# Two encoder layers on eight cores: block products in the feed-forward, a convolution in phase layout, stages without barriers

## Chip, cores, metric

One Trainium2 chip, eight cores. Each core computes one sequence of the batch (4096 positions, 1024 channels) with its own copy of the weights; the cores exchange nothing. The metric is the device time in microseconds of the slowest core.

## What is computed

Matmul operands may be bf16; sums are float32. Per sequence:

```python
# D=1024, SEQ=4096, D_FF=2816
for l in (0, 1):
    h = rmsnorm(x, mix_norm_g[l])
    x = x + (even_mixer(h) if l == 0 else odd_mixer(h))
    h = rmsnorm(x, ffn_norm_g[l])
    x = x + (silu(h @ w_gate[l]) * (h @ w_up[l])) @ w_down[l]
return rmsnorm(x, final_norm_g)

# even_mixer: z = h @ w_in (1536 wide) -> a, gate, p (512 each)
#   ya = silu(layernorm(depthwise_conv31(a * sigmoid(gate)) + b))
#   yb = (mean over a centred window of 2/4/8/16 positions - p) @ pool_w * scale, per group of 128 channels
#   return concat(ya, yb) @ w_out
# odd_mixer: z = h @ w_in -> c, u, v (512 each)
#   yc = Re(DFT over positions and 128 channels of c) @ fourier_w, 4 heads
#   yd = gelu(u) * (W_s @ layernorm(gelu(v)) + b) in chunks of 128 positions
#   return concat(yc, yd) @ w_out
```

## The kernel before

Everything is written out instruction by instruction. Class K issues the work: `mm` (L107, the matmul itself is L111) issues a group of TensorE matmuls that share a PSUM bank, `op` (L100) one instruction of another engine, `dma` (L116, L119) transfers on the queue of SP or of POOL. Each operand has a Dep, and `_pre` (L75) makes the issuing engine wait for the last writer and readers. Engines work in the order of the program text. `run_pipeline` (L274) interleaves the stages of a loop over tiles of 128 positions. `barrier` (L138) makes every engine wait for all engines and all transfers; it stands after each stage, where SBUF memory is given to other tensors.

**mixer0** (L496), one stage after the other: `norm_phase` (L330) reads 32 tiles of x, squares and sums on ACT (L298), takes a root on ACT (L301) and a reciprocal on DVE (L304), scales on DVE (L308), transposes by eight matmuls against `ident` and evacuates into `bigA`; then the projections: a and gate (512 matmuls of 128x512), 124 diagonal weight matrices `diag` built by DVE (L546), p; pooling as matmuls against band matrices; the convolution as 31 matmuls for each of 32 blocks (8 groups of 512 positions times 4 of channels), each against one diagonal matrix that shifts by one tap, with layernorm over channels by matmuls against `ones`; the output projection `out_phase` (L345, add at L369).

**ffn_phase** (L378), once per layer: four supertiles `st` of 1024 positions. `gu(st)` (L406): for 22 columns of 128 hidden channels and 2 halves of 512 positions, eight matmuls for gate and eight for up, then silu on ACT (L430) and the product into `gT` on DVE (L432): 704 matmuls. The weights come as float32 and are cast by transfers on POOL's queue into `wgu`, three slots of 256 columns of gate and up, again for every supertile; `wd` is loaded once. `down_stages(st)` (L436): 8 tiles of 44 matmuls, added to the residual (L460) and stored, woven with the normalisation of the next supertile.

**mixer1** (L693): normalisation; c to memory (`cdr`), u; v with gelu (L775), statistics on DVE (L781, L784), normalisation on ACT (L803) and POOL (L807, L810), product with `swT`; the Fourier transform in three steps of matmuls with evacuations shared by ACT and DVE (`evac_on`, L872); output projection.

One block of gate:

```python
k.mm([(ps[:, bg, :], wgu[:, sl, 0, kk, jj * 128:(jj + 1) * 128],
       hT_[:, kk, tg * 512:(tg + 1) * 512], kk == 0, kk == 7) for kk in range(8)], ...)
```

## Time and profile before

| | us |
|---|---|
| median of 3 runs (3437.47 to 3456.11) | 3439.22 |
| profiled execution, span of the slowest core | 3426.9 |
| spans of the eight cores | 3407.2 to 3426.9 |
| TensorE busy in it | 2912.4 (85%) |
| DVE, ACT, POOL busy | 987.9, 833.8, 310.7 |

The span runs from the first to the last instruction of the core. The profiled execution's own device time isn't listed; the median of the runs is 12.3 us above its span, which is start and end around the instructions. All eight cores do the same, and their mean granted TensorE clock lies at 0.922 to 0.925 of full speed. Busy time of an engine says how long at least one instruction was in it; idle time counts only where it is TensorE's, or where TensorE waits for it.

### The profile page before, as it was taken

Reading aid. Unit: us, or ns where it says so; the run is one execution under the profiler, and the core shown is the slowest. Engines: PE = TensorE matmul, PEld = TensorE weight load, DVE = VectorE, ACT = ScalarE, POOL = GpSimd, SP = SyncE. Lnnn points to the kernel's source line nnn. Section 1 sums busy time; section 2 is a strip of 40 time slices with the busy share of each in tenths; the row PEclk is TensorE's granted clock in tenths of the full one; section 3 lists DMA queues with packets and bytes.
Section 4 is the critical chain, followed back from the end, with each engine's and each line's share of the span. In section 5 each row is a group of like instructions: output and inputs, shape, how many; then the busy total and the mean of one; then the engine's idle time right before and its main releaser. Section 6 shows DMA issues by size and latency. Waiting matters only on the chain.

```text
span 3426.9 us, 42073 instructions; the slowest of 8 cores (3407.2 to 3426.9 us)
## 1 busy us (share of the span) xinstructions
PE 2912.4 (85%) x14392; PEld 1376.4 (40%) x14392; DVE 987.9 (29%) x1566; ACT 833.8 (24%) x1515; POOL 310.7 (9%) x337
## 2 busy tenths in 40 slices
PE   2875999877999999999955966299599899899898
PEld 2433544333444444444433422164244444444444
DVE  5342322341122132221135044153212323323222
ACT  5211344111112211111025345230212212212211
POOL 0000122000101101101000033200110010010000
PEclk9987999988999999999976976599799999999999
DMA  8002000689645635536254000438965465454432
GB/s 217 26 1 34 2 1 1 205 264 165 81 120 103 81 136 88 86 114 81 53 157 157 30 1 1 101 114 286 208 87 110 113 76 122 105 74 123 80 50 80
DMA packets 259436, 336.74 MB, mean 98 GB/s; under 512 B 10784, under 2 KB 199840, under 8 KB 258464
## 3 DMA queue, kind: packets, MB, share of 16 engines
q0 software_dynamic: 196448, 117.62, 25.9%
q1 hardware_dynamic: 62784, 216.43, 18.5%
q8 instruction: 124, 2.03, 0.2%
q14 instruction: 80, 0.66, 0.1%
HBM read 380.31 MB, written 71.30 MB: 132 GB/s over the span
## 4 chain that ended last, share of the span: by engine, by line
PE 79%; DMA 7%; ACT 4%; DVE 4%; issue 4%; POOL 1%; DVEq 0%; SPq 0%; ACTq 0%; POOLq 0%
PE ps L111 79%; DMA sb_wgu<-ffn_w_up 3%; ACT sb_junk L298 2%; DMA sb_xin<-xres 2%; DVE sb_diag L546 1%; DMA sb_fw<-od_fourier_w 1%; ACT sb_vt L803 1%; DVE sb_hb L308 1%; DMA sb_xin<-x 1%; POOL sb_vt L807 1%; DMA sb_band<-band 1%; POOL sb_vn L810 1%; DVE sb_bst L781 0%; ACT sb_vt L775 0%; DMA xres<-sb_xout 0%
## 5 line engine op out<-in xcount | busy, mean ns | idle before, releaser
L111 PE MATMUL ps<-sb_h2T,sb_wgu 128*128 128x512 bf16 x5632 | 1237.6, 383 | 46.9 <-DMA sb_wgu<-ffn_w_up 46.9
L111 PEld LDWEIGHTS ps<-sb_h2T,sb_wgu 128*128 128x128 bf16 x5632 | 556.0, 99 | 725.4 <-issue 74.7
L111 PE MATMUL ps<-sb_wd,sb_gT 128*128 128x512 bf16 x2816 | 613.0, 379 | 10.8 <-DVE sb_gT L432 10.8
L432 DVE TENSOR_TENSOR sb_gT<-sb_tmp,ps 128x512 bf16<-128x512 f32 x352 | 242.1, 688 | 1041.2 <-PE ps L111 1023.6
L111 PE MATMUL ps<-sb_w_in,sb_bigA 128*128 128x512 bf16 x1792 | 426.6, 402 | 51.7 <-DVE sb_p_sb L560 35.7
L430 ACT ACTIVATE sb_tmp<-ps 128x512 f32<-128x512 f32 x352 | 210.1, 597 | 1027.4 <-PE ps L111 1027.3
L111 PEld LDWEIGHTS ps<-sb_wd,sb_gT 128*128 128x128 bf16 x2816 | 273.9, 98 | 339.2 <-issue 14.5
L111 PE MATMUL ps<-sb_ident,sb_hb 128*128 128x128 bf16 x1024 | 114.6, 281 | 237.5 <-DVE sb_hb L308 110.2
L111 PEld LDWEIGHTS ps<-sb_w_in,sb_bigA 128*128 128x128 bf16 x1792 | 180.2, 102 | 280.6 <-issue 89.0
L119 POOL DMA_DIRECT2D sb_wgu<-ffn_w_gate x88 | 77.6, 882 | 1978.4 <-PE ps L111 1643.3
L298 ACT ACTIVATE sb_junk<-sb_xin 128x1024 bf16<-128x1024 f32 x128 | 134.3, 1049 | 357.8 <-DMA sb_xin<-xres 347.3
L111 PE MATMUL ps<-sb_uT,sb_diag 128*128 128x512 bf16 x992 | 215.8, 379 | 1.9 <-DVE sb_bigA L613 1.9
L111 PEld LDWEIGHTS ps<-sb_ident,sb_hb 128*128 128x128 bf16 x1024 | 89.5, 126 | 267.1 <-issue 260.0
L111 PE MATMUL ps<-sb_bigA,sb_w_in 128*128 128x512 bf16 x768 | 168.0, 382 | 2.0 <-issue 2.0
L308 DVE SCALAR_TENSOR_TENSOR sb_hb<-sb_xin,sb_ssb,sb_gbc 128x1024 bf16<-128x1024 f32 x128 | 164.4, 1284 | 14.9 <-DVE sb_ssb L304 3.0
L460 DVE TENSOR_TENSOR sb_xout<-sb_xin,ps 128x1024 f32<-128x1024 f32 x64 | 78.0, 1218 | 233.3 <-PE ps L111 233.3
L111 PEld LDWEIGHTS ps<-sb_uT,sb_diag 128*128 128x128 bf16 x992 | 96.2, 97 | 120.3 <-issue 2.2
L369 DVE TENSOR_TENSOR sb_xout<-sb_xin,ps 128x1024 f32<-128x1024 f32 x64 | 78.2, 1221 | 149.7 <-PE ps L111 126.9
L111 PEld LDWEIGHTS ps<-sb_bigA,sb_w_in 128*128 128x128 bf16 x768 | 75.6, 98 | 94.1 <-issue 4.7
L321 ACT ACTIVATE sb_h2T<-ps 128x512 bf16<-128x512 f32 x64 | 38.1, 595 | 307.3 <-PE ps L111 306.8
L111 PE MATMUL ps<-sb_swT,sb_vn 128*128 128x128 bf16 x128 | 33.9, 265 | 69.6 <-POOL sb_vn L810 58.4
L324 DVE TENSOR_SCALAR sb_h2T<-ps 128x512 bf16<-128x512 f32 x64 | 44.1, 689 | 138.1 <-PE ps L111 138.1
(101 smaller groups left out, 1375.8 us busy)
## 6 DMA issues: line engine op xcount, KB each, us to landing
sb_xin<-xres SPq DMA_DIRECT2D x192, 512.0 KB, 5.5
xres<-sb_xout SPq DMA_DIRECT2D x96, 512.0 KB, 3.7
sb_wgu<-ffn_w_gate POOLq DMA_DIRECT2D x88, 512.0 KB, 6.4
sb_wgu<-ffn_w_up POOLq DMA_DIRECT2D x88, 512.0 KB, 8.3
sb_xin<-x SPq DMA_DIRECT2D x64, 512.0 KB, 5.7
out<-sb_xout SPq DMA_DIRECT2D x32, 512.0 KB, 3.0
sb_wd<-ffn_w_down POOLq DMA_DIRECT2D x4, 2816.0 KB, 73.8
sb_gbc<-norm_g SPq DMA_DIRECT2D x11, 512.0 KB, 4.4
```

Source lines behind the costliest of these rows:

```text
L111: ins = self.nc.tensor.matmul(o, lhsT=l, rhs=r, start=st, stop=sp)
L119: ins = q.e.dma_start(out=o, in_=i)
L298: k.op(act, lambda e: e.activation(out=junk[:], in_=xin[:, xs, :], func=AF.Square, accum_out=ssb[:, s_:s_ + 1]), reads=[d_xin[xs]], writes ...
L308: k.op(dve, lambda e: e.scalar_tensor_tensor(out=hb[:, h_, :], in0=xin[:, xs, :], scalar=ssb[:, s_:s_ + 1], in1=gbc[:, 0, :], op0=ALU.mult ...
L321: k.op(act, lambda e: e.activation(out=hT[:, 0:4, c0:c0 + 128], in_=psv[:, 0:4, :], func=AF.Copy, scale=float(np.sqrt(D))), reads=[psd[b]] ...
L324: k.op(dve, lambda e: e.tensor_scalar(out=hT[:, 4:8, c0:c0 + 128], in0=psv[:, 4:8, :], scalar1=float(np.sqrt(D)), scalar2=None, op0=ALU.mult),
L369: k.op(dve, lambda e: e.tensor_tensor(out=xout[:, xo, :], in0=xin[:, xs, :], in1=ps[:, b:b + 2, :].rearrange("p b n -> p (b n)"), op=ALU.add),
L430: k.op(act, lambda e: e.activation(out=tmp[:, ts_, :], in_=ps[:, bg, :], func=AF.Silu), reads=[psd[bg]], writes=[d_tmp[ts_]])
L432: k.op(dve, lambda e: e.tensor_tensor(out=gT[:, j, tg * 512:(tg + 1) * 512], in0=tmp[:, ts_, :], in1=ps[:, bu, :], op=ALU.mult), reads=[d_ ...
L460: k.op(dve, lambda e: e.tensor_tensor(out=xout[:, xo, :], in0=xin[:, xs, :], in1=ps[:, b:b + 2, :].rearrange("p b n -> p (b n)"), op=ALU.add),
L546: k.op(dve, lambda e: e.tensor_scalar(out=diag[:, c, tap, :], in0=identf[:], scalar1=cw[:, c, tap:tap + 1], scalar2=None, op0=ALU.mult), r ...
L803: k.op(act, lambda e: e.activation(out=vt[:, r_, h * 128:(h + 1) * 128], in_=vt[:, r_, h * 128:(h + 1) * 128], func=AF.Identity, scale=mv[ ...
```

## The change

All stages are rewritten. What it does, by stage:

- **Waits.** `barrier` is gone. SBUF has fixed addresses; `reg` makes a new tensor wait for the last users of exactly those bytes. TensorE no longer waits for its own semaphore.
- **Feed-forward.** The products of 1024 positions with the weights are taken as products of 2x2 blocks with seven block products instead of eight. The contraction (1024 into 2x512), the hidden channels (2x1408) and the positions (2x512) are halved; sums and differences of blocks stand in 7 parts: `hTs` (activations), `slot` (weights), `G` (hidden activations). `gu` has 22 groups (11 pairs of gate and up) of 28 matmuls of 128x512, that is 616, in 7 products of 4; ACT copies running sums out of PSUM (`snap`), DVE adds the other products (`addb`), ACT applies silu in SBUF, DVE multiplies (`mult`) and makes four sums of two bf16 parts (L325). `down` has 28 products of 11 matmuls, 308, each added to `X` in SBUF. The parts of the weights are made once per layer by `Prep`: 33 pieces, each 4 casting loads on POOL's queue, 4 sums and a store to memory; 24 pieces of layer 0 in mixer0 (sums on DVE), 9 in the first `gu` (on POOL), 21 of layer 1 in the next three `gu` (on POOL), 12 in mixer1 (on DVE). The supertiles then read bf16 parts by SP's queue into three slots: 10 loads of 1.84 MB, 2 of 0.92 and 7 of 1.44 per supertile.
- **mixer0.** Positions are ordered by phase (position modulo 8). Normalisation, projections and pooling run as one loop, one tile and 24 matmuls at a step. Pooling is adds on DVE (L325) without matmuls. The convolution runs on 32 groups of 16 channels times 8 phases: 5 matmuls each with matrices `CW` of 640 columns, made by POOL (8 ahead, 24 in the loop); u goes to memory and back for that. The layernorm's two halves run on DVE, POOL and ACT, the first before the output projection, the second woven into it; its result goes to memory and back. The pool weights are multiplied into `w_out`.
- **mixer1.** Normalisation, the three projections, the layernorm of v and the gating are one loop. The layernorm's affine part is on DVE (L1315). The first four tiles are normalised in the last `down` of layer 0.
- **Normalisation** everywhere: sum of squares on ACT (L451), then add and power -0.5 on POOL (L337, L325), then L457 on DVE; no root on ACT, no reciprocal on DVE. Its steps are woven into `down` and into the output projections, with the next stage's first tiles.

```diff
+PRD = {"P1": (0, 0), "P2": (1, 1), "P3": (6, 2), "P4": (2, 6), "P5": (3, 3), "P6": (4, 4), "P7": (5, 5)}
+
+GP = {0: 0, 1: 1, 4: 2, 5: 3, 3: 4, 6: 5, 2: 6}
+
+GL = []
+for _d in range(5):
+    GL += [(0, 2 * _d), (0, 2 * _d + 1), (1, 2 * _d), (1, 2 * _d + 1)]
+GL += [(0, 10), (1, 10)]
...
+                    seq = [(3, 5, 0, ALU.subtract), (4, 2, 3, ALU.subtract), (5, 2, 5, ALU.subtract),
+                           (6, 1, 4, ALU.subtract)]
+                    dst, dd = wds[l].rearrange("s p n -> p s n")[:, :, it[1] * 512:(it[1] + 1) * 512], d_wds[l][it[1]]
+                else:
+                    seq = [(3, 5, 2, ALU.add), (4, 3, 0, ALU.subtract), (5, 0, 5, ALU.subtract),
+                           (6, 1, 4, ALU.subtract)]
...
+                for o, a, c, op in seq:
+                    tt(self.eng, buf[:, o], buf[:, a], buf[:, c], op, d, d)
...
+                def snap(g, x):
+                    v = nx()
+                    grp[g][x] = v
+                    copy_on(act, X[:, v, :], ps[:, grp[g]["A"], :], [psd[grp[g]["A"]]], [dX[v]])
+
+                def addb(g, x, b):
+                    v = grp[g][x]
+                    tt(dve, X[:, v, :], X[:, v, :], ps[:, b, :], ALU.add, [dX[v], psd[b]], [dX[v]])
...
+                for g in range(NJ + 1):
+                    m = g - 1
...
+                        prod(g, "P1", grp[g]["A"], True)
+                        snap(g, "x1")
+                    if m >= 0:
+                        prod(m, "P7", grp[m]["A"], False)
+                        snap(m, "x3")
+                    if g < NJ:
+                        prod(g, "P2", grp[g]["B"], True)
+                        addb(g, "x1", grp[g]["B"])
+                        if not gate_g:
+                            mult(g, "x1", 0)
+                    if m >= 0:
+                        addb(m, "x3", grp[m]["C"])
+                        if not gate_m:
+                            mult(m, "x3", 2)
+                    if g < NJ:
+                        prod(g, "P6", grp[g]["A"], False)
+                        snap(g, "x2")
+                    for a in late:
+                        silu(*a)
+                    late = []
+                    if m >= 0:
+                        A_ = grp[m]["A"]
+                        prod(m, "P4", A_, False)
+                        if gate_m:
+                            v = nx()
+                            grp[m]["x4"] = v
+                            k.op(act, lambda e: e.activation(out=X[:, v, :], in_=ps[:, A_, :], func=AF.Silu),
+                                 reads=[psd[A_]], writes=[dX[v]])
+                            silu(m, "x3")
+                        else:
+                            s4 = grp[PART[m]]["x4"]
+                            jm = GL[m][1]
+                            tt(dve, G[:, GP[1], jm, :], X[:, s4, :], ps[:, A_, :], ALU.mult, [dX[s4], psd[A_]],
+                               [dG[1][jm]])
+                    if g < NJ:
+                        if gate_g:
+                            silu(g, "x1")
+                        prod(g, "P5", grp[g]["C"], True)
+                    if m >= 0:
+                        prod(m, "P3", grp[m]["C"], False)
+                        addb(m, "x2", grp[m]["C"])
+                        if gate_m:
+                            late.append((m, "x2"))
+                        else:
+                            mult(m, "x2", 5)
+                            jp = GL[m][1]
+                            for o, a, b, op in ((3, 5, 2, ALU.add), (4, 3, 0, ALU.subtract), (5, 0, 5, ALU.subtract),
+                                                (6, 1, 4, ALU.subtract)):
+                                tt(dve, G[:, GP[o], jp, :], G[:, GP[a], jp, :], G[:, GP[b], jp, :], op,
+                                   [dG[a][jp], dG[b][jp]], [dG[o][jp]])
...
+                def prod(p, i, b, s, first):
+                    wp = PRD[p][0]
+                    k.mm([(ps[:, b, :], G[:, GP[wp], j, i * 128:(i + 1) * 128],
+                           self.slot[s][:, j * 512:(j + 1) * 512], first and j == 0, j == HJ - 1) for j in range(HJ)],
+                         reads=[self.d_slot[s]] + dG[wp], writes=[psd[b]], more=not first)
...
+        def conv(g):
+            b = k.rot("cv", [0, 1, 2, 3])
+            s = g % NCW
+            k.mm([(ps[:, b, :], CW[s][:, o, :], U[:, g, o:o + NB], o == 0, o == 4) for o in range(5)],
+                 reads=[d_CW[s]] + d_Uq, writes=[psd[b]])
+            v = U[:, g, 2:2 + NB]
+            k.op(act, lambda e: e.activation(out=v, in_=ps[:, b, :], func=AF.Identity, bias=evp[:, g, 0:1]),
+                 reads=[psd[b], d_evp], writes=[d_v[g]])
+            k.op(act, lambda e: e.activation(out=vq[g % 4][:], in_=ps[:, b, :], func=AF.Square, bias=evp[:, g, 0:1]),
+                 reads=[psd[b], d_evp], writes=[d_vq[g % 4]])
+
+        def conv_stat(g):
+            k.mm([(ps[:, 6, :], sel[:], U[:, g, 2:2 + NB], g == 0, g == NG - 1)], reads=[d_sel, d_v[g]],
+                 writes=[psd[6]])
+            k.mm([(ps[:, 7, :], sel[:], vq[g % 4][:], g == 0, g == NG - 1)], reads=[d_sel, d_vq[g % 4]],
+                 writes=[psd[7]])
+
+        for g in range(NG + 2):
...
+        for T_ in range(1, 10):
+            for j in range(4):
+                u = 4 * T_ + j
+                w = u - 4
+                if u < NT:
+                    d_norm(u)
+                if w < NT:
+                    cproj(w)
+                    uproj(T_ - 1, j)
+                    vproj(w)
+                if 0 <= w - 1 < NT:
+                    cstore(w - 1)
+                    vstat(w - 1)
+                if 0 <= w - 2 < NT:
+                    vnorm(w - 2)
+                if 0 <= w - 4 < NT:
+                    sgu(w - 4)
+                if w >= 1 and w % 8 == 1 and w > 1:
+                    ctm_load((w - 9) // 8)
+                if w % 4 == 0 and w < NT:
+                    prep1.step()
```

On DVE, the gate and up part of the first supertile: before, one product per pair of banks (`gT`), between the normalisation and the first add of `down`.

```order
L304 RECIPROCAL sb_ssb<-sb_ssb 128x1
L308 SCALAR_TENSOR_TENSOR sb_hb<-sb_xin,sb_ssb,sb_gbc 128x1024
L324 TENSOR_SCALAR sb_h2T<-ps 128x4x128 x2
L432 TENSOR_TENSOR sb_gT<-sb_tmp,ps 128x512 x44
L460 TENSOR_TENSOR sb_xout<-sb_xin,ps 128x1024
L304 RECIPROCAL sb_ssb<-sb_ssb 128x1
L308 SCALAR_TENSOR_TENSOR sb_hb<-sb_xin,sb_ssb,sb_gbc 128x1024
```

And now, in the first gate and up part, where up groups follow gate groups (`X`: running sums in SBUF, `ps`: PSUM, `G`: the parts of the hidden activation):

```order
L325 TENSOR_TENSOR sb_X<-sb_X,ps 128x512
L325 TENSOR_TENSOR sb_G<-sb_X 128x512
L325 TENSOR_TENSOR sb_G<-sb_X,ps 128x512
L325 TENSOR_TENSOR sb_X<-sb_X,ps 128x512
L325 TENSOR_TENSOR sb_G<-sb_X 128x512
L325 TENSOR_TENSOR sb_G<-sb_G 128x512 x4
L325 TENSOR_TENSOR sb_X<-sb_X,ps 128x512 x2
L325 TENSOR_TENSOR sb_G<-sb_X 128x512
L325 TENSOR_TENSOR sb_G<-sb_X,ps 128x512
L325 TENSOR_TENSOR sb_X<-sb_X,ps 128x512
L325 TENSOR_TENSOR sb_G<-sb_X 128x512
L325 TENSOR_TENSOR sb_G<-sb_G 128x512 x4
```

Each of the 44 products `gT` before is replaced by adds from PSUM, multiplications, and, behind every up group, four sums of `G` with itself.

On PE, the convolution before (`uT`: gated input, `diag`: diagonal matrices, `vb`, `vq`: values and squares for the layernorm):

```order
L111 MATMUL ps<-sb_uT,sb_diag 128x512 x124
L111 MATMUL ps<-sb_vb,sb_ones 128x512 x4
L111 MATMUL ps<-sb_vq,sb_ones 128x512 x4
L111 MATMUL ps<-sb_uT,sb_diag 128x512 x124
L111 MATMUL ps<-sb_vb,sb_ones 128x512 x4
L111 MATMUL ps<-sb_vq,sb_ones 128x512 x4
```

And now (`CW`: phase matrices, `sel`: the sum over channels):

```order
L160 MATMUL ps<-sb_U,sb_CW 128x512 x5
L160 MATMUL ps<-sb_U,sb_sel 128x512
L160 MATMUL ps<-sb_vq,sb_sel 128x512
L160 MATMUL ps<-sb_U,sb_CW 128x512 x5
L160 MATMUL ps<-sb_U,sb_sel 128x512
L160 MATMUL ps<-sb_vq,sb_sel 128x512
L160 MATMUL ps<-sb_U,sb_CW 128x512 x5
```

Where 124 matmuls stood per 512 positions there are 5 per group of 16 channels, 160 for 992 in all, and the 64 for the layernorm are spread between them.

On PE in mixer1, where normalisation had ended before; c and u, then v and the gating:

```order
L111 MATMUL ps<-sb_bigA,sb_w_in 128x512 x256
L111 MATMUL ps<-sb_w_in,sb_bigA 128x512 x56
L111 MATMUL ps<-sb_swT,sb_vn 128x128
L111 MATMUL ps<-sb_sbrow,sb_ones_row 128x128
L111 MATMUL ps<-sb_swT,sb_vn 128x128
L111 MATMUL ps<-sb_sbrow,sb_ones_row 128x128
```

And now, in the loop (`hb` the normalised tile, `w_in` and `hT` the projections, `sbrow` and `swT` the gating):

```order
L160 MATMUL ps<-sb_ident,sb_hb 128x128 x8
L160 MATMUL ps<-sb_w_in_13157,sb_hT_13161 128x512 x8
L160 MATMUL ps<-sb_hT_13161,sb_w_in_13157 128x512 x8
L160 MATMUL ps<-sb_w_in_13157,sb_hT_13161 128x512 x8
L160 MATMUL ps<-sb_sbrow,sb_ones_row 128x512
L160 MATMUL ps<-sb_swT,sb_vn 128x128 x4
L160 MATMUL ps<-sb_ident,sb_hb 128x128 x8
```

The transposes of one tile, 24 projection matmuls of the tiles before it and a gating step now follow one another.

## Rows read from the trace of the kernel before

**Rows 1.** The page: busy time by engine; the chain that ended last, by engine.

```profile
PE 2912.4 (85%) x14392; PEld 1376.4 (40%) x14392; DVE 987.9 (29%) x1566; ACT 833.8 (24%) x1515; POOL 310.7 (9%) x337
...
PE 79%; DMA 7%; ACT 4%; DVE 4%; issue 4%; POOL 1%; DVEq 0%; SPq 0%; ACTq 0%; POOLq 0%
```

**Rows 2.** Stages: stretch, its length, busy of PE, PEld, DVE, ACT, POOL, clock, DMA, GB/s.

```profile
230.00:313.00 83.00, 45.84 (x203) 20.11 (x201) 39.04 (x115) 7.76 (x13) 0.90 (x2) 0.77 0.00 1
...
366.00:624.50 258.50, 229.80 (x1056) 101.87 (x1057) 53.56 (x49) 99.19 (x136) 60.03 (x65) 0.98 0.00 1
...
740.00:837.00 97.00, 51.98 (x256) 25.52 (x256) 24.38 (x36) 24.64 (x46) 12.71 (x14) 0.74 1.06 199
837.00:1757.00 920.00, 892.64 (x4224) 408.44 (x4224) 200.55 (x268) 149.34 (x266) 66.40 (x76) 0.99 0.48 93
1757.00:1857.00 100.00, 32.40 (x257) 24.84 (x258) 64.94 (x96) 61.53 (x129) 1.76 (x2) 0.51 0.74 209
...
1980.00:2180.00 200.00, 126.40 (x464) 49.38 (x462) 77.44 (x279) 96.06 (x178) 83.47 (x70) 0.67 0.02 3
2180.00:2223.00 43.00, 4.52 (x37) 3.60 (x38) 2.07 (x3) 6.84 (x25) 0.49 (x1) 0.50 0.79 189
2223.00:2280.50 57.50, 50.03 (x604) 45.33 (x604) 41.07 (x61) 36.62 (x64) 0.00 (x0) 0.94 0.01 2
```

**Rows 3.** The same view, two dense stretches: gate and up, and mixer0's output projection.

```profile
1042.00:1190.00 148.00, 148.00 (x687) 67.10 (x686) 29.58 (x43) 26.31 (x44) 17.47 (x20) 1.00 0.59 88
...
640.00:730.00 90.00, 90.00 (x419) 40.83 (x418) 31.75 (x26) 0.00 (x0) 0.00 (x0) 1.00 0.89 304
```

**Rows 4.** The chain in order of time (start, us, what): two `down` parts.

```profile
1435.35 78.38 PE ps L111 x392
...
1677.75 76.15 PE ps L111 x352
```

**Rows 5.** Groups by line and shape: operation, count, busy us, mean ns, idle before.

```profile
L111 PE MATMUL ps<-sb_h2T,sb_wgu 128*128 128x512 bf16 x5632 | 1237.6, 383 | 46.9 <-DMA sb_wgu<-ffn_w_up 46.9
...
L432 DVE TENSOR_TENSOR sb_gT<-sb_tmp,ps 128x512 bf16<-128x512 f32 x352 | 242.1, 688 | 1041.2 <-PE ps L111 1023.6 <-ACT sb_tmp L430 9.1 <-ACT sb_junk L298 8.5
L111 PE MATMUL ps<-sb_uT,sb_diag 128*128 128x512 bf16 x992 | 215.8, 379 | 1.9 <-DVE sb_bigA L613 1.9
L430 ACT ACTIVATE sb_tmp<-ps 128x512 f32<-128x512 f32 x352 | 210.1, 597 | 1027.4 <-PE ps L111 1027.3
...
L308 DVE SCALAR_TENSOR_TENSOR sb_hb<-sb_xin,sb_ssb,sb_gbc 128x1024 bf16<-128x1024 f32 x128 | 164.4, 1284 | 14.9 <-DVE sb_ssb L304 3.0
...
L803 ACT ACTIVATE sb_vt<-sb_vt,sb_nmr,sb_mv 128x128 f32<-128x128 f32 x128 | 62.4, 490 | 9.7 <-DVE sb_nmr L794 0.7
...
L807 POOL TENSOR_TENSOR sb_vt<-sb_vt,sb_vln 128x512 f32<-128x512 f32 x32 | 40.4, 1263 | 229.0 <-ACT sb_vt L803 229.0
...
L781 DVE BATCH_NORM_STATS2 sb_bst<-sb_vt 128x6 f32<-128x128 f32 x128 | 37.4, 292 | 68.3 <-ACT sb_vt L775 58.4
L546 DVE TENSOR_SCALAR sb_diag<-sb_identf,sb_cw 128x128 bf16<-128x128 f32 x124 | 35.5, 286 | 13.4 <-DVE sb_diag L546 0.3
...
L784 DVE BATCH_NORM_AGGREGATE sb_mv<-sb_bst 128x2 f32<-128x6 f32 x128 | 23.3, 182 | 13.9 <-DVE sb_mv L784 0.9
```

**Rows 6.** Timeline in mixer1's v loop (start us, us).

```profile
2043.19 3.59 PE L111 MATMUL ps<-sb_w_in,sb_bigA 128*128 128x512 bf16 x8
```

**Rows 7.** DMA queues (packets, MB, share of 16 engines); issues (size, us to landing).

```profile
q0 software_dynamic: 196448, 117.62, 25.9%
...
sb_ctm<-cdr SPq DMA_DIRECT2D x4, 1024.0 KB, 17.2
sb_w_in<-ev_w_in POOLq DMA_DIRECT2D x2, 1536.0 KB, 38.2
```

**Rows 8.** By line: duration of one in ns, min/median/max; first and last start.

```profile
L308 DVE SCALAR_TENSOR_TENSOR sb_hb<-sb_xin,sb_ssb,sb_gbc x128: 1283/1284/1287, 16.8 to 3184.5; 128x1024 bf16<-128x1024 f32 x128
...
L807 POOL TENSOR_TENSOR sb_vt<-sb_vt,sb_vln x32: 1257/1263/1267, 1988.2 to 2171.1; 128x512 f32<-128x512 f32 x32
```

1815 lines of the change are left out of this document (1044 added, 771 removed).

## Prediction

> **What bounds the kernel now.** First the page [rows 1]: TensorE is busy 85% of the span and makes 79% of the chain that ended last; DVE has 29%, ACT 24%, POOL 9%. So time goes away where TensorE gets fewer matmuls or where it stops waiting; work may move to DVE and ACT as long as they stay under it. Then the stages [rows 2]: the feed-forward of layer 0 (837 to 1757) is dense, 892.6 of 920 us, at a granted clock of 0.99. The convolution (366 to 624.5) has 229.8 of 258.5. The rest is where TensorE waits: 37 us for DVE's diagonal matrices and evacuations (230 to 313), 97 us with 52 busy around the first gate and up (740 to 837), 100 us with 32 busy in a normalisation (1757 to 1857), 200 us with 126 busy in the v loop, 43 us with 4.5 busy before the Fourier part. The price of a matmul is read in the dense stretches [rows 3]: 148.00 us for 686 of 128x512, 0.216 us each, at clock 1.00; a transpose among them costs (78.38 - 76.15) / 40 = 0.056 us [rows 4]. Of 14392 matmuls, 5632 are gate and up and 992 the convolution [rows 5]; `down` has 2816.
>
> The sum is made against this execution's span, 3426.9 us; the median of the runs is 12.3 us more, and I add 12 at the end.
>
> **Feed-forward, layer 0.** Per supertile 616 + 308 matmuls replace 704 + 352: 924 x 0.216 = 199.6, with 64 transposes 203.2, four times 813 us. What hides the new work? In gate and up DVE had one product of 0.69 for 16 matmuls (L432) [rows 5]. Now, per gate and up pair (56 matmuls, 12.1 us), it has 6 adds, 4 multiplications and 4 sums of two bf16 parts. An add or a multiplication costs as L432, 0.69. No row shows a sum of two bf16 tiles: the ends are 0.29 (L546, a quarter of the elements) and 0.69 (L432); I take 0.69, the same operation and shape. The order excerpts show that the up groups hold most of it: of four groups (24.2 us of TensorE) two iterations have 11 and 10 operations of DVE, 14.5 us against 12.1 of TensorE, and the others 3 and 4. TensorE's next product waits for the bank that DVE must read, so 2.4 us are lost per four groups, 5.5 x 2.4 = 13 per supertile, 53 per layer; at the lower end, nothing. ACT's 6 copies and 4 silus at 0.60 (L430) are 6 of 12.1 us. In `down` one add of 0.69 stands against 11 matmuls, 2.4 us; the woven normalisation needs up to 1.28 (L308) + 0.69 + 4 x 0.69 at every third product and fits within two. The power on POOL has no row; between 0.29 and 1.26 us, with a tile of lead, it is hidden, and DVE's next add would pay if it were not. DMA per supertile: 30.3 MB of weight parts, 12.6 of x, 6.9 of stores of parts, at the 304 GB/s of [rows 3] 164 us, and 3.9 MB of casting loads at q0's 117.62 MB / (0.259 x 3427 us) = 132 GB/s [rows 7], 30 us: 194 of 216. It fits, narrowly. All of it but the casts is in SP's one queue, in order: a weight load that waits for its slot holds the loads and stores of x behind it, and `down` then waits for those; I add 10. Sum 876, for 1017 before (740 to 1757).
>
> By the Trainium skill (VectorE: DVE Perf Modes, "The perf-mode tier table"), adding two bf16 tensors in SBUF runs at twice the rate, 1224 ns for 2048 elements. An estimate from that page would be 0.42 us here. No row shows such an operation; it is the second case below.
>
> **mixer0.** Start: `w_in` landed after 38 us [rows 7], and the first projections need two thirds of it: 33. Loop: 768 matmuls (166) and 256 transposes (14): 180. Pooling falls on DVE in three bursts of some 20 us beside 10 us of other work, in rounds of 23 us: 12. The last u goes to memory and back under 64 matmuls: 5 us show, between 0 and the 17.2 us of a 1 MB round trip [rows 7]. Convolution: 224 matmuls, 48 us, replace 1056. ACT has 32 x 1.4 us, but POOL's 24 matrices of 640 elements cost 1.263 x 640/512 = 1.58 each (L807), with 11 times 2.2 of load issues: 62 us. Then TensorE stands still: the root and reciprocals, 16 steps of the layernorm's first half, where ACT has 32 silus between L803's 0.49 (128 wide) and L430's 0.60, 18 us, and the trip through memory: 40. Output projection 512 x 0.216 = 110.6, and 18 for the next normalisation's last tiles. Sum 460, for 740 before.
>
> **mixer1.** A tile has 24 matmuls, 8 transposes, a gating step: 6.1 us. DVE has 1.28 (L308) + 4 x 0.29 (L781) + 4 x 0.18 (L784) + 4 x 0.29 (as L546) + 0.69, and 0.69 for the weight parts: 5.7. So 32 x 6.1 = 195 replace the normalisation, the projections and the v loop, 423 (1757 to 2180). The last c goes through memory: 12 (between 5 and 17.2). The Fourier part is kept: 57 [rows 2]. Output 110.6 + 14. Sum 389, for 636 before.
>
> **Feed-forward, layer 1.** 813 + 53, and the final norm: DVE waits for ACT's square and POOL's root in its place in the queue, some 6 us per supertile: 24; 8 at the end. Sum 898, for 1033.
>
> 460 + 876 + 389 + 898 = 2623, with 12: **2635 us**.
>
> **The rivals.**
> - *DVE stays under TensorE.* If the bf16 sums take 0.42, the up iterations need 12.3 us against 12.1; with one late bank of 0.6 that is 0.8 per four groups, 4 per supertile, and 8 x 9 = 70 us go: 2565. For it: DVE's rows of float32 say nothing against it. Chance 0.27.
> - *POOL and DVE hold each other up.* 30 pieces have their 4 sums on POOL (1.26 each, L807) in layer 0, where DVE has 4.9 us free in 24.2; if each waits for the other where both operands are in SBUF, about 40 us are added there, 25 in the convolution and layernorm, 40 in mixer1, where POOL's two operations per tile meet 0.4 us of slack: 2740. Against it: L308, with two operands in SBUF, and L807 hardly spread, 1283 to 1287 and 1257 to 1267 ns [rows 8], but no row has both at once. Chance 0.17. The Trainium skill (SBUF — State Buffer, "Who interferes with whom") states exactly this, an exclusive lock on a shared port pair; no row here shows it.
> - *Transfers bind in layer 0.* At 250 GB/s instead of 304 the 49.8 MB take 199 us and the casting loads 30, 229 for 216: +52, and waits for single slots: 2700. For it, 1.06 of DMA at 740 to 837 [rows 2] moved only 199 GB/s. Chance 0.06.
> - *It isn't without barriers.* If the waits for reused bytes act as the barriers did, the gaps of [rows 2] stay in part, some 120 us: 2755. Chance 0.05.
> - *Half clock: slower than before.* TensorE now pauses for a bank after every few products of four matmuls. In the v loop, where it waited 3 to 4 us between groups, eight matmuls took 3.59 us [rows 6], 0.449 each, the 1.2 GHz level, and that stage's clock was 0.67. If the gate and up matmuls, 4928, ran so, they would cost 0.233 us more each, 1148 us: 3783. It decides from some 3500 matmuls on. Against it: the pauses worked out above are 0.6 to 2.4 us among 24 us of work, and in the dense stages with pauses between banks the clock stayed at 0.98. Chance 0.02. The Trainium skill (TensorE: Matmul & The Clock Gate, "A second HAM failure mode") says that cycling through PSUM banks can make the clock fall again and again; the trace disagrees for this kernel's gate and up, where the clock was 1.00 with eight banks in turn [rows 3].
>
> **How the numbers follow.** The forecast as summed has 0.42, and 0.01 is left for no change. A measurement of this kernel tells about 0.5%, 17 us, from nothing. Range: the second case less what I may have overpriced (45 us in the layernorm's gap, the convolution and the final norm) is 2520; the lock with 40 us of transfers is 2780. Faster 0.97, within 0.5% 0.01, slower 0.02.
>
> **What would show it.** A supertile's gate and up at 146 us and `down` at 67; 133 would make the second case right. TensorE's waits in gate and up named DVE's adds and products; sums of two bf16 parts at 0.69 or below; the convolution near 62 with waits for POOL's `CW`; one gap of about 40 before the output projection; a mean clock of at least 0.95. Wrong: DVE operations that last over 1 us beside POOL's sums, waits for `slot`, matmuls of gate and up at 0.43, or a mixer1 loop over 210 us.

## The result, and the profile after

The median of five runs is 2870.11 us (2864.15 to 3009.84); before, 3439.22. The direction was right, but the forecast of 2635 (2520 to 2780) was 235 us too low. Some executions of every kernel, before included, ran several per cent longer with one die's clock lowered, so each ratio, time and median from here on is of the others alone: for the changed kernel 2869.14 us and a ratio of 0.8334, with a 95% interval of 0.8302 to 0.8365.

The page of the changed kernel's slowest core, which answers to [rows 1]:

```profile
span 2862.8 us, 39898 instructions; the slowest of 8 cores (2844.9 to 2862.8 us)
PE 2409.7 (84%) x11785; PEld 1117.9 (39%) x12008; DVE 1672.0 (58%) x2704; ACT 1000.8 (35%) x1799; POOL 697.9 (24%) x918
DMA  8898659969689779779797556784463465464452
PE 53%; DVE 19%; issue 11%; DMA 9%; ACT 3%; POOL 2%; SPq 2%; DVEq 1%; ACTq 0%; POOLq 0%
```

TensorE lost 503 us of busy time and the span 564. But the chain of work that ended last has in part changed hands: 79% of it was TensorE's, now 53%, with DVE at 19% where it had 4%.

The stages (stretch, its length, busy of PE, PEld, DVE, ACT, POOL, clock, DMA, GB/s): mixer0's loop, convolution, standstill, output projection; the first gate and up and its `down`; mixer1's loop with its tail, and its Fourier part; the first and second gate and up of layer 1.

```profile
33.00:259.00 226.00, 190.43 (x969) 89.15 (x987) 134.09 (x189) 95.89 (x184) 68.99 (x104) 0.96 0.86 161
259.00:346.00 87.00, 57.51 (x220) 23.45 (x224) 54.68 (x63) 40.24 (x64) 53.83 (x56) 0.84 0.70 146
346.00:427.00 81.00, 3.98 (x8) 0.86 (x8) 31.75 (x42) 25.88 (x48) 27.56 (x27) 0.51 0.62 117
427.00:601.00 174.00, 124.38 (x566) 56.96 (x579) 80.13 (x98) 29.66 (x56) 30.43 (x44) 0.84 0.93 277
601.00:764.00 163.00, 140.39 (x604) 60.36 (x616) 98.78 (x155) 65.68 (x115) 60.41 (x68) 0.94 0.76 210
764.00:834.00 70.00, 69.63 (x367) 33.69 (x372) 38.89 (x64) 10.99 (x20) 5.00 (x12) 1.00 0.73 261
1491.00:1732.00 241.00, 206.92 (x1136) 98.12 (x1155) 186.26 (x471) 109.19 (x205) 182.92 (x221) 0.95 0.63 152
1732.00:1804.00 72.00, 56.34 (x630) 49.66 (x629) 49.10 (x84) 43.79 (x87) 6.94 (x14) 0.88 0.75 174
1932.00:2071.00 139.00, 134.45 (x603) 59.39 (x614) 89.56 (x155) 66.51 (x116) 2.54 (x4) 0.99 0.41 143
2149.00:2304.00 155.00, 136.59 (x604) 59.74 (x616) 96.28 (x162) 69.32 (x123) 5.70 (x12) 0.94 0.44 154
```

Read against the terms of the forecast, with the remaining supertiles from the first matmul of each part:

| us | forecast | measured |
|---|---|---|
| start | 33 | 33 |
| mixer0: loop, pooling, last u | 197 | 226 |
| convolution, with the wait behind it | 62 | 87 + 27 |
| layernorm's first half | 40 | 54 |
| output projection, normalisation | 129 | 174 |
| layer 0: gate and up | 585 | 163 + 150 + 147 + 151 = 611 |
| layer 0: `down` | 291 | 3 x 70 + 69 = 279 |
| mixer1: loop, last tiles | 207 | 241 |
| Fourier part | 57 | 72 |
| output projection, normalisation | 125 | 128 |
| layer 1: gate and up | 585 | 139 + 155 + 155 + 154 = 603 |
| layer 1: `down`, final norm, end | 313 | 78 + 77 + 77 + 95 = 327 |

Of the 238 us between the columns, 140 lie ahead of the first gate and up. Five readings say where to look.

**TensorE stands behind a scaling of four small tiles.** The waits of TensorE, then of POOL, in the convolution and what follows (us in all, times, longest); then DVE's and TensorE's timelines there (start, us, what, in brackets the idle time before and what ended it):

```profile
PE ps L160 <- DVE sb_pw L1066: 28.2, 1, 28.2
PE ps L160 <- POOL sb_CW L915: 27.6, 5, 9.9
POOL sb_prep L168 <- DMA gud<-sb_prep: 32.6, 6, 9.6
```

```profile
353.13 2.01 DVE L325 TENSOR_TENSOR sb_prep<-sb_prep 128x512 bf16<-128x512 bf16 x4 [10.29 <-DMA sb_prep<-ffn_w_gate]
355.53 2.01 DVE L325 TENSOR_TENSOR sb_prep<-sb_prep 128x512 bf16<-128x512 bf16 x4 [0.39 <-DMA sb_prep<-ffn_w_up]
369.62 2.01 DVE L325 TENSOR_TENSOR sb_prep<-sb_prep 128x512 bf16<-128x512 bf16 x4 [12.08 <-DMA sb_prep<-ffn_w_up]
371.55 1.33 DVE L1066 TENSOR_SCALAR sb_pw<-sb_pw,sb_pscale 128x128 bf16<-128x128 bf16 x4
...
373.13 2.81 PE L160 MATMUL ps<-sb_w_lo,sb_pw 128*128 128x512 bf16 x6 [28.22 <-DVE sb_pw L1066]
```

The scaling takes 1.3 us, but it is queued behind the sums of the last weight pieces. Those wait for their load; POOL issues the load only when the buffer's earlier store has landed; and the convolution's matrices `CW` stand behind the same loads in POOL's queue. The releaser that the profile names (DVE) is the last link of a chain of transfers.

**The casting loads are dear.** DMA queues (packets, MB, share of 16 engines) in the stretch 350 to 372, then over the whole span:

```profile
q0 software_dynamic: 4818, 1.90, 81.5%
q1 hardware_dynamic: 288, 1.84, 21.5%
...
q1 hardware_dynamic: 185360, 524.82, 56.4%
q0 software_dynamic: 71248, 47.76, 13.3%
```

For 1.90 MB the casting queue takes 81.5% of 22 us, 106 GB/s of a full share, where [rows 7] gave me 132; over the whole span it is 125, and 325 for the plain queue. A piece of 0.5 MB is then 4 to 5 us of all 16 engines, and its 0.9 MB store 3 more.

**DVE and POOL hold each other up.** Durations in ns, min/median/max, first DVE in the second gate and up of layer 0, then a DVE product and a POOL sum in mixer1's loop, the same POOL sum before, and DVE's sums of weight parts in the convolution; last, DVE's and POOL's timelines there:

```profile
L325 DVE TENSOR_TENSOR sb_G<-sb_G x40: 417/424/1372, 858.6 to 976.3; 128x512 bf16<-128x512 bf16 x40
L325 DVE TENSOR_TENSOR sb_G<-sb_X x32: 691/693/1561, 847.3 to 982.5; 128x512 bf16<-128x512 f32 x32
L325 DVE TENSOR_TENSOR sb_X<-sb_X,ps x66: 672/681/689, 834.2 to 981.8; 128x512 f32<-128x512 f32 x66
...
L457 DVE SCALAR_TENSOR_TENSOR sb_hb<-sb_xin,sb_rsb,sb_gbc x24: 1275/1976/1983, 1500.0 to 1680.3; 128x1024 bf16<-128x1024 f32 x24
L325 POOL TENSOR_TENSOR sb_vn<-sb_vt,sb_vln x26: 1261/2000/2069, 1512.2 to 1696.9; 128x512 bf16<-128x512 f32 x26
...
L810 POOL TENSOR_TENSOR sb_vn<-sb_vt,sb_vln x32: 1259/1262/1267, 1989.6 to 2172.6; 128x512 bf16<-128x512 f32 x32
...
L325 DVE TENSOR_TENSOR sb_prep<-sb_prep x44: 418/425/4841, 260.4 to 371.2; 128x512 bf16<-128x512 bf16 x44
...
288.46 6.42 DVE L325 TENSOR_TENSOR sb_prep<-sb_prep 128x512 bf16<-128x512 bf16 x4
290.84 3.75 POOL L915 TENSOR_TENSOR sb_CW<-sb_convv,sb_mask 128x640 bf16<-128x640 f32 x3
```

The adds with an operand in PSUM never spread; those with both in SBUF last up to 0.95 us longer in this gate and up. Before, the same POOL addition had 1.26 us every time. In the convolution one DVE sum lasted 4.84 us, and it ended 0.3 us after three POOL products in a row (294.88 and 294.59). A sum of two bf16 tiles is 0.42 us when nothing disturbs it: the value of my second case.

**The final norm stops DVE for 2.7 us per tile**, here at the end of a `down`, and TensorE's next wait in the gate and up behind it:

```profile
2383.68 1.28 DVE L746 SCALAR_TENSOR_TENSOR sb_X<-sb_X,sb_rsb,sb_gbc 128x1024 f32<-128x1024 f32 x1 [2.68 <-POOL sb_rsb L325]
2384.88 0.68 DVE L325 TENSOR_TENSOR sb_X<-sb_X,ps 128x512 f32<-128x512 f32 x1
...
2388.24 1.28 DVE L746 SCALAR_TENSOR_TENSOR sb_X<-sb_X,sb_rsb,sb_gbc 128x1024 f32<-128x1024 f32 x1 [2.68 <-POOL sb_rsb L325]
...
2392.40 1.87 PE L160 MATMUL ps<-sb_hTs,sb_slot 128*128 128x512 bf16 x4 [9.84 <-DVE sb_X L325]
```

A tile costs DVE 4.6 us here, while TensorE has a bank ready every 2.4, the time of 11 matmuls.

**The power stands behind the pieces.** POOL, then DVE, in the first gate and up:

```profile
707.14 2.17 POOL L168 DMA_DIRECT2D sb_G<-ffn_w_down  x4 [5.41 <-DMA wds<-sb_G]
709.32 5.04 POOL L325 TENSOR_TENSOR sb_G<-sb_G 128x512 bf16<-128x512 bf16 x4
714.45 0.22 POOL L337 TENSOR_SCALAR sb_rsb<-sb_ssb 128x1 f32<-128x1 f32 x1
...
715.49 1.28 DVE L457 SCALAR_TENSOR_TENSOR sb_hb<-sb_xin,sb_rsb,sb_gbc 128x1024 bf16<-128x1024 f32 x1 [12.21 <-POOL sb_rsb L325]
```

### The profile page after: what moved, and what is told of

Its sections match the earlier page's. It is cut to its first block, busy times and chain, and to the rows that moved or that the text cites. A ratio compares the mean times of both kernels' runs of the same rounds, so it can differ in the third digit from the quotient of the medians.

```text
span 2862.8 us, 39898 instructions; the slowest of 8 cores (2844.9 to 2862.8 us)
## 1 busy us (share of the span) xinstructions
PE 2409.7 (84%) x11785; PEld 1117.9 (39%) x12008; DVE 1672.0 (58%) x2704; ACT 1000.8 (35%) x1799; POOL 697.9 (24%) x918
## 3 DMA queue, kind: packets, MB, share of 16 engines
q1 hardware_dynamic: 185360, 524.82, 56.4%
q0 software_dynamic: 71248, 47.76, 13.3%
## 4 chain that ended last, share of the span: by engine, by line
PE 53%; DVE 19%; issue 11%; DMA 9%; ACT 3%; POOL 2%; SPq 2%; DVEq 1%; ACTq 0%; POOLq 0%
PE ps L160 53%; DVE sb_X L325 5%; DVE sb_G L325 4%; DVE sb_hb L457 2%; DVE sb_Wt L325 2%; DMA sb_prep<-ffn_w_up 2%; SPq L168 2%; DVE sb_prep L325 2%; DMA sb_xin<-x 1%; DMA sb_xo<-x 1%; DVE sb_vt L1315 1%; DVE sb_bst L1302 1%; ACT sb_G L742 1%; DMA gud<-sb_prep 1%; DMA xres<-sb_xo 1%
## 5 line engine op out<-in xcount | busy, mean ns | idle before, releaser
L160 PE MATMUL ps<-sb_hTs,sb_slot 128*128 128x512 bf16 x4826 | 1092.6, 383 | 122.6 <-DVE sb_X L325 71.4
L325 DVE TENSOR_TENSOR sb_X<-sb_X,ps 128x512 f32<-128x512 f32 x752 | 507.1, 683 | 585.7 <-PE ps L160 570.7
L160 PEld LDWEIGHTS ps<-sb_hTs,sb_slot 128*128 128x128 bf16 x4928 | 476.4, 98 | 737.5 <-issue 209.4
L160 PE MATMUL ps<-sb_slot,sb_G 128*128 128x512 bf16 x2410 | 543.2, 381 | 23.0 <-DVE sb_X L325 19.9
L329 ACT ACTIVATE sb_X<-ps 128x512 f32<-128x512 f32 x528 | 314.9, 597 | 597.7 <-PE ps L160 592.4
L337 POOL TENSOR_SCALAR sb_rsb<-sb_ssb 128x1 f32<-128x1 f32 x160 | 52.7, 330 | 1472.1 <-ACT sb_hb L451 912.6
L160 PEld LDWEIGHTS ps<-sb_slot,sb_G 128*128 128x128 bf16 x2464 | 239.3, 98 | 304.1 <-issue 30.5
L160 PE MATMUL ps<-sb_hT,sb_w_in 128*128 128x512 bf16 x996 | 240.9, 391 | 27.9 <-DVE sb_ucm L325 18.5
L325 DVE TENSOR_TENSOR sb_G<-sb_X 128x512 bf16<-128x512 f32 x264 | 202.1, 765 | 30.8 <-DVE sb_X L325 6.3
L457 DVE SCALAR_TENSOR_TENSOR sb_hb<-sb_xin,sb_rsb,sb_gbc 128x1024 bf16<-128x1024 f32 x112 | 155.6, 1390 | 75.6 <-POOL sb_rsb L325 73.9
L635 ACT ACTIVATE sb_X<-sb_X 128x512 f32<-128x512 f32 x264 | 160.6, 624 | 32.3 <-DVE sb_X L325 32.2
L325 DVE TENSOR_TENSOR sb_xo<-sb_xo,ps 128x1024 f32<-128x1024 f32 x64 | 78.0, 1219 | 159.2 <-PE ps L160 95.4
L325 DVE TENSOR_TENSOR sb_G<-sb_G 128x512 bf16<-128x512 bf16 x352 | 158.5, 491 | 18.7 <-DVE sb_G L325 0.6
L325 POOL TENSOR_TENSOR sb_G<-sb_G 128x512 bf16<-128x512 bf16 x120 | 148.1, 1234 | 74.9 <-DMA sb_G<-ffn_w_up 34.7
L325 POOL TENSOR_TENSOR sb_rsb<-sb_rsb,sb_mhalf 128x1 f32<-128x1 f32 (+1 forms) x192 | 135.4, 705 | 29.1 <-POOL sb_rsb L337 1.1
L325 DVE TENSOR_TENSOR sb_prep<-sb_prep 128x512 bf16<-128x512 bf16 x144 | 89.8, 624 | 67.8 <-DMA sb_prep<-ffn_w_up 41.0
```

The costliest lines, as they stand in the source:

```text
L160: ins = self.nc.tensor.matmul(o, lhsT=l, rhs=r, start=st, stop=sp, skip_group_check=more)
L325: return k.op(eng, lambda e: e.tensor_tensor(out=o, in0=a, in1=b, op=op), reads=reads, writes=writes)
L329: k.op(act, lambda e: e.activation(out=o, in_=i, func=AF.Copy), reads=reads, writes=writes)
L337: k.op(pool, lambda e: e.tensor_scalar(out=o, in0=i, scalar1=float(eps), scalar2=None, op0=ALU.add), reads=[d_i], writes=[d_o])
L457: k.op(dve, lambda e: e.scalar_tensor_tensor(out=self.hb[h][:], in0=x[:], scalar=rsb[:, c, 0:1], in1=gbc[self.gi][:], op0=ALU.mult, op1=AL ...
L635: k.op(act, lambda e: e.activation(out=X[:, v, :], in_=X[:, v, :], func=AF.Silu), reads=[dX[v]], writes=[dX[v]])
```

## The experiments

Every one is an edit of the changed kernel, with its name ahead of it; the times compare with its 2869. Stages are measured from the first matmul of one to that of the next. What differs without an edit says how much to read: the runs were made in five series, in which the kernel before had medians of 3430 to 3439 us, so under 10 us between two series is nothing. In the eleven profiles with an unchanged first mixer, the changed kernel's own included, the first gate and up starts at 584 to 601 us (median 596; the changed kernel's 601 is the latest). In the twelve with unchanged gate and ups of layer 0 these take 606 to 630 us in sum, where the changed kernel has 611. The first gate and up of layer 1 takes 138 to 140 where nothing in it is changed.

### The pieces in the first mixer

**m0_no_parts** (loads and sums left out, stores kept):

```diff
 def step(self, more=True):
+    if self.l == 0 and self.eng is dve:
+        ...
+        self.store(); return
```

> Leaves out the loads and the sums of the 24 weight pieces that the first mixer prepares (each store is kept and writes zeros, so layer 0's feed-forward multiplies zeros there). Theory P (each piece is a load, four sums and a store in two buffers, and POOL and DVE wait for it at a fixed place in their queues): the loop from 33 to 259 us falls from 226 to about 200, the convolution from 87 to about 62, the standstill behind it from 81 to about 45, and the output projection with the last normalisations from 174 to about 150; the first gate and up starts near 490 instead of 601 and the run takes about 2760. Theory L (POOL and DVE hold each other up where both work in SBUF, and the pieces only add DVE work to that): no more than 25 us of the 601 go, nearly all of it in the convolution and the layernorm.

2773.85 us, one run: 95 less. Loop 207, convolution 49, no wait behind it, layernorm 54, output 155; the first gate and up at 500, 101 earlier than in the changed kernel and 96 earlier than the median. In the convolution and in the output projection:

```profile
241.00:290.00 49.00, 48.73 (x226) 21.68 (x225) 38.80 (x33) 40.91 (x65) 39.02 (x26) 1.00 0.73 214
344.00:500.00 156.00, 124.21 (x578) 56.46 (x579) 75.56 (x82) 29.77 (x56) 23.58 (x32) 0.88 0.92 287
```

The convolution is now TensorE's own 224 matmuls. So the 62 us that I had given to POOL's matrices were too many: eight are built ahead, and the rest fits. DVE's operations were held up by POOL here too (its sums on `Wt` reached 1.86 us, none wider than 786 columns), and TensorE didn't wait for them: the hold alone isn't what the convolution pays. This run alone can't tell waits from transfers, since it removes both; the stores' transfers stay.

**m0_spread:**

```diff
-            if g % 3 == 2:
+            if g % 8 == 5:
                 prep0.step()
...
-                if t % 4 == 0 and prep.n < nprep:
+                if t % (2 if lg is not None else 4) == 0 and prep.n < nprep:
```

> The same 24 pieces with the same transfers, but 4 steps in the convolution instead of 11, and one at every second tile of the output projection instead of every fourth. Theory P: the convolution falls from 87 to about 65 and the 28 us wait for the scaled pooling weights to under 8; the output projection gives back at most 10; the run is 30 to 45 us shorter. Theory D (the transfers themselves bind, at a DMA share of 0.7 to 1.0): the same bytes take the same time, within 10 us of 2870.

2868.99 us (ratio 0.834, 0.8319 to 0.8361): nothing. Convolution and wait fell from 114 to 61, further than theory P said, and the output projection rose from 174 to 222. Both theories were half right: what the convolution had paid, the output projection pays now, with the DMA share at 0.95; whether in waits or in transfers this run doesn't tell:

```profile
376.00:598.00 222.00, 135.40 (x572) 58.38 (x573) 90.82 (x125) 29.41 (x55) 50.41 (x72) 0.80 0.95 262
```

**m0_three** (a third buffer for the pieces, and the scaling of the pooling weights, L1066, ahead of the convolution):

```diff
+        prep0.b.append(k.buf("prep", 67840, [128, 7, 512], BF16)[:])
+        ...
+        for g in range(4): ...
         def conv(g):
```

> The pieces of the convolution get a third buffer, and the scaling of the pooling weights moves ahead of the convolution on DVE; the same 24 pieces at nearly the same steps. Theory P: convolution and wait together fall from 114 to 75 to 90 us, the output projection keeps its 174, the run is 20 to 40 us shorter. Theory D (the casting loads' transfers bind, whatever waits for them): the convolution stays within 8 us of 87 and the run within 12 us of 2870.

2830.10 and 2837.75 us: 35 less, or 28 if it is allowed for that the kernel before took 3432 in this series. Convolution and wait 78, layernorm 62 where it had 54, output 170. TensorE's wait for the scaling (28.2 us) is gone, that for `CW` is 20.8 instead of 27.6. The same transfers at nearly the same place cost some 30 us less, so this part of the waits in the convolution was a matter of buffers and queue order. The third buffer and the moved scaling weren't tried apart.

**out_half_x:**

```diff
+                w_ = D if t < 8 or self.src_deps else D // 2
-                k.dma(sp, [(self.xo[s][:], self.load(t))], ...
+                k.dma(sp, [(self.xo[s][:, 0:w_], self.load(t)[:, 0:w_])], ...
```

> In the output projection of the first mixer the residual x of the tiles from 8 on is loaded only in its first 512 columns (the rest keeps what the buffer held); the first mixer's output is another there. Theory D (transfers bind: 1 MB per tile against 3.46 us of TensorE, at a DMA share of 0.99): 24 tiles save 0.25 MB each, 20 us at 300 GB/s, and the stretch from its first product to the first gate and up falls from 174 to 155 to 162 us. Rival P (it waits only for the pieces and the last layernorm half, whatever is moved): above 168.

2836.87 us, one run. The stretch fell from 174 to 151 (169 to 179 in the eleven profiles), for 6.3 MB less (24 tiles of 0.26 MB), 21 us at 300 GB/s. The middle of the stretch still moves 300 GB/s at a DMA share of 1.00:

```profile
480.00:540.00 60.00, 53.04 (x238) 23.45 (x237) 19.91 (x19) 2.30 (x4) 3.77 (x8) 0.91 1.00 300
```

Theory D holds for this stage, if a little more came than it said: per tile it moves 1 MB, 3.4 us, beside 3.46 us of TensorE, and each piece comes on top.

### The gate and up of layer 0

**gu_sums_dve:**

```diff
-                    prep.bufs(..., [[dG[p][c] for p in range(7)] for c in cols], pool)
+                    prep.bufs(..., [[dG[p][c] for p in range(7)] for c in cols], dve)
```

> The 120 sums of weight parts in the gate and up of layer 0 run on DVE instead of POOL; loads and stores stay. Theory L (a DVE operation with both operands in SBUF waits for the end of a POOL operation): no DVE operation of these stretches lasts over 0.75 us, and the gate and up of supertiles 2 to 4 fall from 147 to 151 us to 141 to 144, the run by 15 to 30 us. Rival (DVE's load is what counts, 120 x 0.42 us more on it, and its waits for the loads in its queue): the gate and up rise above 150 and the run is 5 to 30 us longer.

2873.50 us (ratio 0.8358, 0.8334 to 0.8383), 4 more, which is no difference: the intervals overlap. Gate and up 165, 151, 152, 156, in sum 624, inside the 606 to 630 of unchanged profiles. The first half of the expectation came, the second did not:

```profile
L325 DVE TENSOR_TENSOR sb_G<-sb_G x68: 416/425/427, 855.6 to 974.8; 128x512 bf16<-128x512 bf16 x68
L325 DVE TENSOR_TENSOR sb_G<-sb_X x32: 691/692/694, 845.3 to 981.0; 128x512 bf16<-128x512 f32 x32
```

The spread is gone with POOL's sums: the hold is real. But nothing was gained by ending it. That DVE's own 0.42 us per sum costs as much as the hold did would explain it; the next two runs look at each alone.

**gu_pool_alone:**

```diff
+                    if self.last and st == 0: ...
+                        for _ in range(2): tt(pool, G[:, 1, 10, :], G[:, 0, 10, :], G[:, 0, 10, :], ALU.add, ...)
```

> Adds 28 sums of two bf16 tiles on POOL, which nothing waits for, to the first gate and up of layer 1 (139 us, where POOL has nothing to do); no transfer, no piece, no store is added. Theory L (POOL and DVE hold each other up where all operands are in SBUF): DVE's products and sums without a PSUM operand go up to 1.2 to 1.6 us there, its adds with a PSUM operand stay below 0.70, and the gate and up takes 144 to 148 us. Rival Q (what the pieces cost in layer 0 comes from their transfers and from waits in the queues): it stays at 139 to 140 us. The run changes by the same few us.

141 us for 139 (2862.21 us in all): between the two theories, nearer to Q. DVE's products there:

```profile
L325 DVE TENSOR_TENSOR sb_G<-sb_X x32: 691/692/1445, 1941.3 to 2066.0; 128x512 bf16<-128x512 f32 x32
```

They reached 1.45 us, the adds from PSUM 0.69. The hold alone is worth about 2 us per supertile here, in one profile.

**gu_dve_alone:**

```diff
+                        for _ in range(4): tt(dve, G[:, 1, 10, :], G[:, 0, 10, :], G[:, 0, 10, :], ALU.add, ...)
```

> Adds 28 sums of two bf16 tiles on DVE (7 times 4, 0.42 us each, 11.8 us in all), whose data nobody waits for, to the first gate and up of layer 1 (139 us). If DVE's time in the up iterations goes to TensorE nearly one to one, it takes 145 to 151 us, which explains why moving the pieces' sums from POOL to DVE gained nothing. If the 45 us in which DVE is free there take them up, it stays at 139 to 142, and what layer 0 pays beyond that is the pieces' waits.

145 us for 139: half of the 11.8 us of added DVE work is paid by TensorE, though DVE is free for a third of the time. The likely reason is that DVE's free time lies in the steps with 3 or 4 of its operations, while all seven bursts of four sums stand right behind a step with 10 of them or right ahead of one with 11. No run puts them elsewhere, so this isn't shown.

**gu_0_7_14:**

```diff
-P1_FFN = (7, 7, 7)
+P1_FFN = (0, 7, 14)
```

> The 21 pieces of layer 1 that are prepared in gate and up of supertiles 2 to 4 of layer 0 are dealt 0, 7 and 14 instead of 7, 7 and 7. If a piece has one price, gate and up take about 140, 149 and 159 us, and the run stays within 5 us. Rival (the extra 10 us of layer 0 over layer 1 have another source, the stores and loads of x or the weight parts read while others are written): the supertile with no piece still takes over 146 us.

139, 145 and 211 us (2902.07 in all). Without a piece, layer 0 runs as layer 1 does, so the pieces are the whole difference. But a piece has no fixed price: with 14 the gate and up takes 211 where 159 was expected, and the loads no longer land in time. What ended waits there, the longest of each at the end:

```profile
POOL sb_G L325 <- DMA sb_G<-ffn_w_up: 41.3, 4, 21.0
PE ps L160 <- DVE sb_X L325: 33.5, 7, 27.1
DVE sb_hb L457 <- POOL sb_rsb L325: 28.3, 2, 28.1
PE ps L160 <- DMA sb_slot<-gud: 26.6, 3, 13.9
```

It is the chain of the fifth reading, now 28 us long: load, POOL's sum, the power behind it, DVE's product, TensorE's bank. And here TensorE waits another 26.6 us for weight parts in `slot`.

**hooks:**

```diff
-                        if nm is not None and g in (9, 13, 14, 15):
+                        if nm is not None and g in (7, 9, 14, 18):
```

> The first four steps of the next normalisation are issued at groups 7, 9, 14 and 18 of gate and up instead of 9, 13, 14 and 15, so that the square and the power lie five groups ahead of the product that needs them. Theory P (POOL's power stands behind a piece's sums and loads in POOL's queue, DVE's product waits for it in its place, TensorE waits 12 us for DVE in supertile 1): the first gate and up falls from 163 to 150 to 153 us, supertiles 2 to 4 by 0 to 3 each, the run by 10 to 18. Rival: the 12 us come back in the same gate and up at the next bank, because POOL is late by as much there: 160 or more.

2842.69 us, one run, but 17 of the 26 us lie ahead of the first gate and up, which this edit doesn't touch, and the kernel before took 3430 in this series. The gate and ups: 160, 153, 149, 145, in sum 607, 4 less and inside the scatter. The 12 us wait was replaced by one of 6 us for the last piece's store, which DVE's next sum needs. The expectation missed; the rival was nearer.

### The final norm

**fn_late** (with it, all due entries of `later` are issued at once, not one per product):

```diff
-                    k.op(dve, lambda e: e.scalar_tensor_tensor(out=xv, ...
+                    later.append([1, lambda: k.op(dve, lambda e: e.scalar_tensor_tensor(out=xv, ...
```

> The product of the final normalisation is issued behind the next product of the down matrix instead of at once behind the square and the power. Theory F (DVE stands 2.7 us per tile in its place in the queue, eight tiles per supertile, while TensorE needs 2.4 us per product): down falls from 77.5 to about 71 us, the following gate and up from 154 to about 141, three times; the run is 50 to 65 us shorter. Rival (the next supertile waits for X buffers that the stores to out still read): under 15 us.

2809.07 us (ratio 0.8153, 0.8129 to 0.8176): 60 less, as expected. `down` 74, 74, 73 for 78, 77, 77, the gate and up behind them 144, 142, 142 for 155, 155, 154, the last `down` with the end 81 for 95: 62 in sum. DVE's product no longer stands idle in its place:

```profile
2370.59 1.28 DVE L746 SCALAR_TENSOR_TENSOR sb_X<-sb_X,sb_rsb,sb_gbc 128x1024 f32<-128x1024 f32 x1
```

### The second mixer's loop

**v_no_affine:**

```diff
-                                                    ... out=vt[r][:, hs], in0=vt[r][:, hs], ...
+                                                    ... out=vn[n][:, hs], in0=vt[r][:, hs], ...
-            tt(pool, vt[r][:], vt[r][:], vln[:, 0, :], ALU.mult, ...)
-            tt(pool, vn[n][:], vt[r][:], vln[:, 1, :], ALU.add, ...)
```

> Leaves out the two affine steps of v's normalisation (POOL's product and sum); DVE writes the normalised tile. Theory L (POOL at 4.6 us per tile, and 0.7 us of DVE's 2.0 spent waiting for it, set the pace): loop and tail of the second mixer fall from 241 to 205 to 215 us. Rival (ACT, or the loads of x, set it): above 228.

2839.10 us; loop and tail 216 for 241, and DVE's product of the normalisation is back at 1.28 us. The stretch in the changed kernel and here, in the columns of the stages, and that product here:

```profile
1500.00:1700.00 200.00, 179.43 (x991) 85.02 (x1009) 158.13 (x397) 97.02 (x183) 149.68 (x178) 0.97 0.64 155
...
1525.00:1680.00 155.00, 153.79 (x878) 73.63 (x893) 126.32 (x363) 83.71 (x156) 65.19 (x112) 0.99 0.62 162
L457 DVE SCALAR_TENSOR_TENSOR sb_hb<-sb_xin,sb_rsb,sb_gbc x21: 1274/1276/1285, 1527.7 to 1657.1; 128x1024 bf16<-128x1024 f32 x21
```

Theory L, at the edge of its range: POOL's work, with what DVE waits for it, is 25 of the 34 us over the forecast. Without it TensorE is busy all the time. With it DVE is busy 158 of 200 us and waits 13; the other 29 are pauses of under 0.15 us between its 397 instructions, so it had next to no time left.

**v_dve:**

```diff
-            tt(pool, vt[r][:], ...); tt(pool, vn[n][:], ...)
+            tt(dve, vt[r][:], ...); tt(dve, vn[n][:], ...)
```

> The two affine steps of v's normalisation in the second mixer run on DVE instead of POOL. Theory L: DVE's product of the normalisation falls from 1.98 to 1.28 us and its affine steps cost 0.69 each instead of 1.3 and 2.0 on POOL; DVE then has about 6.3 us per tile, and the loop (1491 to 1732) falls from 241 to 220 to 230 us, the run by 10 to 20. Rival (DVE becomes the bound, 1.4 us more per tile): the loop rises to 250 or more.

2882.79 us (ratio 0.8389, 0.8334 to 0.8444), 14 more, loop 263: the rival. Nothing spreads any more (1.28, 0.69, 0.69), but DVE now has 1.28 + 4 x 0.29 + 4 x 0.18 + 4 x 0.35 + 3 x 0.69 + 0.42 = 7.1 us per tile, where I had reckoned 6.3; L1315 at 0.35 is 0.2 of the difference. A tile takes 8.2: between 1500 and 1700 us DVE is busy 160 us and waits 8, and its short pauses are 32, 1.3 us per tile.

**v_half_act:**

```diff
-            for h in range(4):
+            for h in (2, 3): ... k.op(act, ... func=AF.Identity, scale=rsb[...], bias=mv[...])
+            for h in range(2):
                 k.op(dve, lambda e: e.tensor_scalar(
```

> Two of the four heads of v's normalisation go from DVE (0.346 us each) to ACT, with one small DVE product per tile (0.18). DVE has 0.5 us less per tile, ACT 1.0 more. If DVE sets the pace of the second mixer's loop (6.9 us per tile), the loop falls from 241 to 222 to 230 us. If POOL and its hold on DVE set it, it stays above 236.

2879.02 us, loop 256: worse than either theory. ACT waited for DVE's new small product (76.7 us in 175) and DVE then for ACT (31.2 us), since both halves write one tile and are ordered. The edit added a dependency, so it says nothing on who sets the pace.

**m1_tail:**

```diff
+                if T_ == 4: m3_head(j)
-                if 0 <= w - 4 < NT:
+                if 0 <= w - 4 < NT - 2:
                     sgu(w - 4)
...
+        sgu(NT - 2); sgu(NT - 1)
```

> In the second mixer the scaled matrices of the Fourier part are built during the loop, and the last two products of the gating step are issued behind the first eight groups of the Fourier part. If the 20 us with TensorE idle at 1712 to 1742 are the chain of the last v tiles in TensorE's queue, the stretch from the first projection to the output projection (313 us) falls by 10 to 18 us. If they are the trip of the last c through memory, it stays within 4 us.

2852.62 us. From the first projection to the output projection 305 for 313: 8 less, short of the 10 to 18, where profiles with an unchanged second mixer have 310 to 316. The part that went is the wait for the matrices (5.7 us) and for the last two tiles; 6.9 us of waits for the tiles before them stayed.

### Together

The edits of fn_late, m0_three, hooks and m1_tail in one kernel.

> The late product of the final normalisation, the third piece buffer with the earlier scaling, the earlier steps of the next normalisation and the changed tail of the second mixer together. If the gains add (57 + 27 measured, 14 + 14 expected): 2740 to 2770 us. If they share one cause or give back in the transfers of the output projection: above 2790.

2749.57 us (ratio 0.8019, 0.7998 to 0.8039), 120 less than the changed kernel, or 108 by the ratios to the kernel before. Convolution and wait 78, gate and ups of layer 1 139, 141, 140, 143. Of the 115 us between the two profiles 37 lie ahead of the first gate and up, 11 in layer 0, 2 in the second mixer and 65 in layer 1. From the first projection to the output projection it takes 312, so the edit of m1_tail, with 14 in the expectation, gave nothing here. This kernel computes the whole result and is faster than both.

## Why the prediction was wrong, step by step

**What held.** The matmul counts and their price: `down` at 70, an undisturbed gate and up at 139. No barrier gaps were left beyond the one foreseen. Slots made TensorE wait for 0.3 us in all, so transfers did not bind in layer 0's feed-forward as dealt. The half clock did not come: the gate and up matmuls have a mean of 383 ns, as before [rows 5], and the clock is 0.94 to 1.00 where they run. The mean clock was 0.94, just under the 0.95 that I asked for; it is low where TensorE stands still. Of my signs of being wrong two came: DVE operations of over 1 us beside POOL's sums, and a mixer1 loop over 210.

**The step that failed: weight pieces in mixer0, costed at nothing but POOL's load issues.** The text has "11 times 2.2 of load issues" for POOL in the convolution; DVE's sums of the pieces stand only in mixer1's 5.7 us, and POOL's in a rival for layer 0. I counted instructions and left out what stands between them: the sum waits for a load and the next load for a store, each in a fixed place of an in-order queue. Leaving the pieces out gave back 101 us: 19 in the loop, 65 in the convolution and behind it, 18 in the output projection (rounded; 96 in all against the median of the eleven profiles). m0_three shows that some 30 of them were waits that other buffers and another order avoid. Their transfers, in a stage where 1 MB per tile already fills TensorE's 3.46 us, were not in the sum either: I looked for the DMA bound in layer 0 alone.

**The final norm, sized 24 us.** The mechanism was named, "DVE waits for ACT's square and POOL's root in its place in the queue", with 6 us per supertile. The edit that takes it away gave 60. I had counted a few waits, not that tiles at 4.6 us meet products at 2.4, and that the backlog runs into the next gate and up.

**mixer1's loop, 6.1 us per tile.** It took 6.9, tail left aside (1491 to 1712 for 32 tiles). Two terms were mis-sized: the affine steps L1315 at 0.29 took 0.35 (0.37 with the hold), and L308's successor at 1.28 took 1.98. A third was left out: the short pauses between DVE's instructions, 29 us in 200, so that the 0.4 us of slack that I gave DVE per tile wasn't there. The third case had the mechanism and 40 us for it in mixer1; v_no_affine shows 25. The last tiles take 18 us (1712.5 to 1730.6) with four waits of 2.7 to 3.6 us, where I had 12 for c's trip. The Fourier part's 15 us over its 57 were not looked into, but for 5.7 us of waits for its matrices.

**The bf16 sum, 0.69.** It takes 0.42, the lower case. Gate and up without pieces is 139, where the main case had 146 and that rival 137. That gave 7 us per supertile back, and in layer 0 the pieces took it again, and more: 153 on average, 14 over 139. The Trainium skill (VectorE: DVE Perf Modes, "The perf-mode tier table") had led to the estimate of 0.42; the trace agrees, with a median of 0.424.

**POOL and DVE.** The rival was right that they wait for each other (1.98 for 1.28 us) and wrong on the price in layer 0: about 2 us per supertile against 10. The Trainium skill (SBUF — State Buffer, "Who interferes with whom") says that a DVE instruction contends with one of GpSimd that reads SBUF if it has two SBUF inputs or runs in a two-port mode, and that the later one blocks for the whole of the other's instruction. The trace agrees that adds with a PSUM operand are free of it: they stayed at 672 to 689 ns. On the length it shows more than one instruction: a sum of 0.42 us lasted 4.84 us, to the end of POOL's third product in a row.

**Loop, convolution and layernorm of mixer0.** For pooling the text has 20 and 10 us of DVE's work in rounds of 23, three times, which is 21 us, but puts down 12; without pieces the loop took 207 where I had 197. The convolution's 62 was too high, 49 without pieces. The gap's 40 was 54 in nearly every run: from the last silu at 412.3 to TensorE's start at 427.3 there are 15 us of trip through memory.

In sum: +101 for the pieces in mixer0, +36 for the final norm (60, with 24 foreseen) and +25 for POOL in mixer1, 162 of the 238 us. In the gate and ups of layer 0 the pieces cost 55 more (611 against four times 139), and the bf16 sums gave back 29 there. The rest is terms of either sign that no run takes apart. The output projection's excess without pieces (155 against 129) is likely transfers, at a DMA share of 0.92; out_half_x shows what they cost with pieces, and without them it wasn't tried. Not tried either: how much of the loop's remaining 10 us in mixer0 is pooling or u's trip, and a gate and up whose up groups carry less of DVE's work.

## What to carry over

A background task of transfers and sums, cut into steps between the steps of other work, costs nothing only if every wait in it is over before its turn comes; in-order queues hand each late load to whatever stands behind it, here a 1.3 us scaling and a power. Cost it by its round trip and its buffers, not by its busy time, and ask of each stage that takes a step whether its transfers are full already. An engine that is free a third of the time can still hold the others up if its work falls into every other group: sum it per iteration, with the short pauses between its instructions (here 0.07 us each), and for a normalisation per tile against the products beside it.

## What was unexpected in the hardware

- The casting queue moved 1.90 MB at 81.5% of 16 engines in 22 us, 106 GB/s of a full share, and 125 over the whole span (47.76 MB at 13.3%), where the plain queue has 325 (524.82 MB at 56.4%).
- DVE and POOL, with all operands in SBUF, can hold each other up for more than one instruction: a DVE sum of 0.42 us lasted 4.84 us beside three POOL products of 1.3 us in a row.
- A normalising step on 128x128 float32 with two per-partition scalars takes DVE 346 ns, also with bf16 output, where a statistics step on the same tile takes 294 and the sum of two bf16 tiles of four times the width 424.
- POOL's power costs 0.6 us for one column and 1.2 for four (97.0 us for 160, 38.4 for 32, waits for DVE included), so it grows with the columns.
